# Stick-breaking prompt attention: the scores' lead, the first value product of a group, and the places of sigmoids and gates in line

## The reference

```
def _sb_block(q, qpos, k, v, kpos):
    scale = HEAD_DIM ** -0.5
    z = jnp.einsum('bqhd,bkhd->bhqk', q, k, preferred_element_type=jnp.float32) * scale
    causal = kpos[None, :] < qpos[:, None]
    log_keep = jnp.where(causal, jax.nn.log_sigmoid(-z), 0.0)
    rev = lax.cumsum(log_keep, axis=log_keep.ndim - 1, reverse=True)
    after = jnp.concatenate([rev[..., 1:], jnp.zeros_like(rev[..., :1])], axis=-1)
    log_a = jnp.where(causal, jax.nn.log_sigmoid(z) + after, -jnp.inf)
    a = jnp.exp(log_a)
    o = jnp.einsum('bhqk,bkhd->bqhd', a, v.astype(jnp.float32))
...
            h = (jax.nn.silu(z) * o.reshape(b, T, D_ATTN)) @ b_w_out[j]
```

## Time and profile before

| | |
|---|---|
| median of 3 runs | 2952.95 us (2952.86 to 2952.97) |
| the profiled execution | 2958.83 us, of which its span is 2957.2 us |
| PE busy over the span | 2848.7 us, 96% |
| DVE, ACT, POOL busy | 1652.0, 1344.4, 1159.3 us |
| attention, first score to last value product | 1453.7 to 2664.6 us |
| one pair in the middle (heads 6 and 7) | 1933.3 to 2087.6 us |

### The profile page before, as it was taken

How to read it: one execution, slowest core, us unless ns; L and a number is a source line. 1 busy time by engine, 2 the same in 40 slices (tenths; PEclk the granted TensorE clock), 3 DMA queues, 4 the chain that set the end, 5 groups by cost and what they waited for, 6 DMA issues and landing times. The chain is left out here.

```text
span 2957.2 us, 42069 instructions
## 1 busy us (share of the span) xinstructions
PE 2848.7 (96%) x14856; PEld 2470.5 (84%) x14856; DVE 1652.0 (56%) x2150; ACT 1344.4 (45%) x2746; POOL 1159.3 (39%) x1023
## 2 busy tenths in 40 slices
PE   7999999999999999999999999999999999998998
PEld 6999999999888888899788888888888877777886
DVE  5322123212443511022488888888888899897774
ACT  6000010100134511111377777777777788785442
POOL 3333233332110110022367666666667576662010
PEclk9999999999999999999999999999999999999999
DMA  5011111011344344244786767675767677857773
GB/s 159 30 33 33 36 36 34 24 36 37 116 150 128 118 173 177 105 148 158 219 243 182 229 183 230 185 226 177 235 176 221 201 213 223 258 182 214 238 226 112
DMA packets 286311, 451.16 MB, mean 153 GB/s; under 512 B 52898, under 2 KB 223010, under 8 KB 280132
## 3 DMA queue, kind: packets, MB, share of 16 engines
q1 hardware_dynamic: 275108, 409.23, 45.5%
q0 software_dynamic: 11040, 39.86, 4.5%
HBM read 325.22 MB, written 123.81 MB: 152 GB/s over the span
## 5 line engine op out<-in xcount | busy, mean ns | idle before, releaser
L1731 POOL TENSOR_TENSOR a_a<-a_a,a_prod 128x512 f32<-128x512 f32 (+3 forms) x640 | 664.8, 1049 | 423.1 <-DVE a_prod L1681 286.7
L1681 DVE TENSOR_TENSOR_SCAN a_prod<-a_keep,a_prod,a_restart 128x513 f32<-128x513 f32 x384 | 488.6, 1273 | 0.1
L1691 DVE TENSOR_TENSOR a_atl<-a_pt,a_ath 128x512 fp32r<-128x512 f32 (+3 forms) x640 | 380.4, 599 | 128.6 <-ACT a_ath L1631 125.1
L1621 ACT ACTIVATE a_a<-a_pz 128x512 f32<-128x512 f32 (+3 forms) x640 | 352.5, 551 | 179.2 <-PE a_pz L1544 166.4
L1631 ACT ACTIVATE a_ath<-a_pt 128x512 fp32r<-128x512 f32 (+3 forms) x640 | 349.2, 556 | 96.2 <-PE a_pt L1569 94.9
L1569 PE MATMUL a_pt<-ident,a_a 128*128 128x128 f32 x2176 | 346.1, 275 | 12.3 <-DVE a_atl L1691 6.9
L1622 ACT ACTIVATE a_keep<-a_pz 128x512 f32<-128x512 f32 (+3 forms) x640 | 354.0, 553 | 0.0
L1569 PEld LDWEIGHTS a_pt<-ident,a_a 128*128 128x128 f32 x2176 | 274.8, 141 | 69.6 <-POOL a_a L1731 14.9
L1554 PE MATMUL a_po<-a_ath,a_v 128*128 128x512 f32 (+3 forms) x640 | 288.8, 451 | 41.8 <-DVE a_atl L1691 21.2
L1543 PE MATMUL a_pz<-a_kh,a_q 128*128 128x512 f32 (+3 forms) x640 | 240.9, 378 | 11.8 <-ACT a_keep L1622 9.4
L277 POOL TENSOR_TENSOR w_wh<-w_raw,w_gain 128x1024 fp32r<-128x1024 f32 x22 | 42.1, 1911 | 536.1 <-PE v_pg L347 279.9
(11 more groups left out here) (233 smaller groups left out, 6079.1 us busy)
## 6 DMA issues: line engine op xcount, KB each, us to landing
a_x<-x_d SPq DMA_DIRECT2D x96, 896.0 KB, 4.7
a_x<-x_d SPq DMA_DIRECT2D x64, 832.0 KB, 4.7
a_kh<-kh_t SPq DMA_DIRECT2D x32, 512.0 KB, 10.8
a_kl<-kl_t SPq DMA_DIRECT2D x32, 512.0 KB, 14.2
w_raw<-in_a_w_in POOLq DMA_DIRECT2D x30, 512.0 KB, 4.8
x<-f_xn POOLq DMA_DIRECT2D x17, 512.0 KB, 6.0
g_y_in<-sz_t SPq DMA_DIRECT2D x17, 512.0 KB, 7.6
g_x<-x SPq DMA_DIRECT2D x17, 512.0 KB, 3.7
```

The lines of the kernel that those rows point to most:

```text
L1621: act.activation(a[:, s, q, 0:w], pz[:, n % ZS, 0:w], ACT.Sigmoid, scale=SCALE)
L1681: dve.tensor_tensor_scan(prod[:, s, 0:w + 1][:, ::-1], keep[:, n % KS, 0:w + 1][:, ::-1], restart[:, 0:1].broadcast_to([P, w + 1]), prod[: ...
L1691: dve.tensor_tensor(atl[:, b % AS, c0:], pt[:, turn_slot(hh, b), c0:], ath[:, b % AS, c0:].bitcast(F32), ALU.subtract).then_inc(at_split, 1)
L1731: pool.tensor_tensor(part, part, prod[:, n % PS, after:after + w], ALU.mult).then_inc(weighted, 1)
```

## The change

The lead goes from 3800 to 4300 columns, so PE's scores stand 500 columns (about one piece of 512) further ahead. How far each engine's part is put back is now in two tables: for score work ACT goes from 0 to 150, DVE stays at 600, POOL goes from 900 to 200, SP stays at 1000; for gates ACT and DVE go from 300 to 250, SP from 1000 to 1500. The product of the first block of each query group stands three blocks behind the transposes instead of two, directly ahead of the product of the second block. The chunks are moved: they begin at column 800 instead of 0 in an ordinary pair (2250 instead of 2000 in the pairs that only have the gate projection), and the last one stands nearer the pair's end. Nothing that is computed changes, nor any count of instructions.

```diff
-LEAD = 3800
-PE_AT, ACT_AT, DVE_AT, POOL_AT, SP_AT = 0, 0, 600, 900, 1000
+LEAD = 4300
+BEHIND = {"PE": 0, "ACT": 150, "DVE": 600, "POOL": 200, "SP": 1000}
+GATE_BEHIND = {"PE": 0, "ACT": 250, "DVE": 250, "POOL": 0, "SP": 1500}
...
+def begins_group(b):
+
+    return is_diagonal(BLOCKS[b][0]) and BLOCKS[b][1] == 0
+
...
-    first = 300 if is_pair(pr, 0) else 2000 if gates(pr) == (Z,) else 0
-    end = HEAD if is_pair(pr, NPAIR - 1) else 2 * HEAD - 1500
-    return [(first + (k + 0.5) * (end - first) / len(out), *x) for k, x in enumerate(out) if x[2] < PARTS]
+    first = 2250 if gates(pr) == (Z,) else 800
+    end = HEAD if is_pair(pr, NPAIR - 1) else 2 * HEAD - 750
+    return [(first + (k + 0.9) * (end - first) / len(out), *x) for k, x in enumerate(out) if x[2] < PARTS]
...
-            items.append((at + (300 if behind < SP_AT else 1000), 3, "gate", m, gx))
+            items.append((at + gate_behind, 3, "gate", m, gx))
...
-                before = lagged(pr, hh, b, LAG)
-                if before:
-                    multiply(*before)
+                for lag in (LAG + 1, LAG):
+                    before = lagged(pr, hh, b, lag)
+                    if before and begins_group(before[2]) == (lag > LAG):
+                        multiply(*before)
```

More of the change, by code:

```diff
@@ L1249, in chunks, with schedule @@
     out = [(gx, m, part) for gx in range(len(PGROUPS)) for m in gates(pr) for part in range(PARTS + 1)]
-    first = 300 if is_pair(pr, 0) else 2000 if gates(pr) == (Z,) else 0
-    end = HEAD if is_pair(pr, NPAIR - 1) else 2 * HEAD - 1500
-    return [(first + (k + 0.5) * (end - first) / len(out), *x) for k, x in enumerate(out) if x[2] < PARTS]
-def schedule(pr, behind):
+    first = 2250 if gates(pr) == (Z,) else 800
+    end = HEAD if is_pair(pr, NPAIR - 1) else 2 * HEAD - 750
+    return [(first + (k + 0.9) * (end - first) / len(out), *x) for k, x in enumerate(out) if x[2] < PARTS]
+def schedule(pr, who):
     last = is_pair(pr, NPAIR - 1)
+    behind, gate_behind = BEHIND[who], GATE_BEHIND[who]
     end = 2 * HEAD - 1
@@ L1399, in lagged, with all_pairs @@
             return None if is_pair(pr, 0) else (pr - 1, 1, N_BLOCK + b - k)
-        def all_pairs(eng, behind, do):
-            for what, hh, n in schedule(-1, behind):
+        def all_pairs(who, do):
+            for what, hh, n in schedule(-1, who):
                 if what == "score ahead":
@@ L1407, in all_pairs, with one_pair @@
             for pr in range(NPAIR):
-                one_pair(pr, behind, do)
-        def one_pair(pr, behind, do):
-            for what, hh, n in schedule(pr, behind):
+                one_pair(pr, who, do)
+        def one_pair(pr, who, do):
+            for what, hh, n in schedule(pr, who):
                 if what == "score ahead":
@@ L1521, in _ @@
             load_v(0, 1)
-            all_pairs(sp, SP_AT, do)
+            all_pairs("SP", do)
         @block.tensor
@@ L1604, in do @@
                     chunk(pr, *hh, n)
-            all_pairs(pe, PE_AT, do)
+            all_pairs("PE", do)
             for b in range(N_BLOCK - LAG, N_BLOCK):
@@ L1659, in do @@
                     project_out(pr, hh, n)
-            all_pairs(act, ACT_AT, do)
+            all_pairs("ACT", do)
             for b in range(N_BLOCK - LAG, N_BLOCK):
@@ L1717, in _ @@
             dve.wait_ge(restart_set, 2)
-            all_pairs(dve, DVE_AT, do)
+            all_pairs("DVE", do)
         @block.gpsimd
@@ L1777, in _ @@
                 pool.sem_inc(done, 2)
-            all_pairs(pool, POOL_AT, do)
+            all_pairs("POOL", do)
     return o_sb
```

## The result

The changed kernel takes 2902.51 us (median of 4 runs, 2899.85 to 2905.56) against 2952.96: a ratio of 0.9825, with a 95% interval of 0.9808 to 0.9842. That is -50.5 us where -27 was forecast; the time lies just under the lower end of the range and within 3 us of the first rival (2905). The direction and most of the places were right; the sum was about half of what came.

What follows compares the result with a forecast made beforehand. PE was taken as the bound, DVE close behind. Pairs 1 to 5 -13.1, pair 0 -2.9, pairs 6 and 7 -4.4, clock -6.8 made -27.2 us: 2952.95 to 2926; own range 2911 to 2944, with rivals 2904 to 2955.

Steps and rivals of the forecast that it cites:

- first rival: Whole kernel: more waits and clock falls go than the forecast counts, -48 us to 2905; chance 0.12.
- product 19, odd heads: Block 19 of odd heads: a gate and scan no longer stand ahead of it on DVE; 5 x 1.5, -7.5 us.
- short scores of group 0: Short scores of group 0: a chunk between them ends PE's waits for sigmoids, -6.1 us.
- short scores in blocks 28 to 30: Odd heads, next head's short scores: the 512-wide score waits for sigmoids behind ACT's copies; 5 x 1.5, +7.5 us.
- end of an even head: Products 37 and 38: block 38 moves ahead of a scan, a gate behind block 37; 5 x -0.7, -3.5 us.
- end of a pair and start of the next: Pair ends: the scan wait goes, missing fill adds 0.9; 1.6 instead of 2.1 us each, -2.5 over five.
- ACT's place costed at nothing: Stretches between the diagonal ones: scores keep the same gap between blocks on PE, ACT and DVE; cost nothing.
- sigmoids rival: Stretches of short scores: PE stands for sigmoids that ACT runs later, +20 us to 2973; chance 0.13.
- SP costed at nothing: SP's queue: gate stores move 500 columns back, some 2 us, and loads behind are asked for later; nothing.
- Clock: Clock falls: four of seven go, the start's, one behind block 19, two at pair ends; 4 x 1.7, -6.8 us.
- rival in which the clock falls more often at head ends: A fall at each of 16 head ends makes the clock term +15.3 instead of -6.8 us, 2948; chance 0.08.
- Pair 0: Pair 0: POOL wait at block 8 goes (-2.1), a chunk runs behind (+1.2), other terms -2.0; sum -2.9 us.

Runs made afterwards that it cites:

- e9: The kernel before with ACT's score work put 150 columns back and nothing else; ratio 0.9932 to the kernel before.
- e7: The changed kernel with ACT's score work back at 0 columns behind instead of 150; ratio 0.9909 to the kernel before.
- e13: The changed kernel with the old chunk places and SP's six key and query loads 2600 columns later in its line; ratio 0.9821 to the kernel before.
- e5: The changed kernel with the old chunk places; ratio 0.9887 to the kernel before.
- e6: The changed kernel without the deferral, a group's first product back at two blocks; ratio 0.9824 to the kernel before.
- e12: The changed kernel with the lead back at 3800 columns; ratio 0.9932 to the kernel before.
- e14: The changed kernel with POOL's score work back at 900 columns behind; ratio 0.9842 to the kernel before.
- e3: The kernel before with the lead at 4300 columns and nothing else; ratio 0.9967 to the kernel before.

## Why the prediction was wrong

**The size of pairs 1 to 5.** The forecast was -13.1 of waits and most of -6.8 of clock; measured were -32.5 and -6.8 (four falls, all of those pairs). The step that failed above all is the one that costed ACT's new place at nothing; beside it the sum was made from a list that holds too little, and the pair end was judged by DVE's busy share. By place, on PE's own list (us over pairs 1 to 5, rounded):

| place | before | forecast | measured change |
|---|---|---|---|
| product 19, odd heads | 7.4 | -7.5 | -7.4 |
| short scores of group 0 | 6.1 | -6.1 | -6.1 |
| short scores in blocks 28 to 30 | 0 | +7.5 | +3.4 |
| end of an even head | 5.9 | -3.5 | -5.9 |
| end of a pair and start of the next | 10.7 | -2.5 | -7.1 |
| other first products | 2.1 | -1.0 | -2.1 |
| x loads | 2.1 | 0 | +0.3 |
| sum | 34.2 | -13.1 | -24.9 |

*The list.* The sum was made from PE's list, 34.2 us, and PE's busy time was taken for work. The weight loads' list of the same stretch had 54.1, 20 us more, and fell by 32.5, 7.6 more than PE's own.

*ACT's place costed at nothing.* "On PE, ACT and DVE a score stands in the same gap between two blocks as before" was true where a gap is 512 columns wide, and I let it stand for the whole. The 150 columns of ACT appear in my text only as the cause of the slower rival. Alone they are worth more than any other part tried (e9: 0.68%), and 0.82% in the whole (e7): at the narrow blocks and at gates they put ACT's short copy ahead of the pair of sigmoids. The changed kernel without them (e7) is what I had forecast for all of it: 0.9909, some 27 us less than before, with 21.4 us left on PE's list, 12.8 less than before. That both sums meet so well is in part luck, since the terms behind them differ, and since parts do not add up here it does not make the 150 columns the whole error. But undone they cost 0.82%, 24 us, and 23 us is what the forecast lacks. The sigmoids rival's own mark, `a_keep` waits above 15 us, did not come: they went from 6.1 to 3.4 on PE's list. DVE's 1.68 us for ACT's gate stood in the earlier trace rows and I used it for one place alone; there were 30 such waits.

*The pair end.* 2.1 us were to become 1.6, since no chunk is left there and DVE was the bound. Measured is one wait of 0.55 for the accumulator and, at product 2 of the new head, one of 0.22:

```profile
2052.75 0.51 PE L1561 MATMUL a_po<-a_ath,a_v 128*128 128x512 f32 x1 [0.55 <-ACT a_o L1649]
2058.86 0.39 PE L1561 MATMUL a_po<-a_ath,a_v 128*128 128x256 f32 x1 [0.22 <-DVE a_atl L1699]
```

The same kernel without ACT's 150 (e7) has there, beside 0.54, still 0.70 at transposes 0. The 0.9 that I added for missing fill was too much. With the old chunks there (e13) the weight loads' waits from the transposes of block 38 to product 2 of the new head are 1.8 us a pair (0.59 and 0.97 for `a_atl`, 0.23 for `a_o`), without them 2.2 (0.79 and 0.39 for `a_o`; 0.20, 0.37 and 0.45 for `a_atl`), and on PE's list they are 0.9 and 0.8: the fill moved the waits more than it covered them. What bounded the stretch was ACT's and DVE's order.

Two sums of the range were wrong as well. The pair end's upper value of 4.0 counts the 0.9 twice (0.7 + 2.4 is 3.1), and the lower end, all of it taken together, is 2913 and not 2911.

**Short scores.** +1.5 in one odd place per pair was forecast; the place was right to the block, its price 0.7 us, 3.4 over five pairs instead of 7.5. The old ones at group 0 went, as said.

**SP costed at nothing.** Right for the changed kernel and wrong as a reading of it: an x load needed 18 us behind six key loads, and the chunks at a pair's start were held off only by the waits themselves (the earlier trace rows has 2.1 us already, at the third chunk of two pairs) and, with the change, by the 1000 columns that its chunks moved. I had costed that move as harmful. Undone, it costs 0.60% (e5), and e13 shows that the loads are why. Even so the changed kernel keeps 2.2 us of waits for x, now at the first chunk.

**The deferral.** "Hardly helps" was right: e6 shows no loss. "POOL, nothing" is not contradicted: 0.15% is below what the runs tell. The lead was costed at nothing, and that was wrong: alone it is worth 0.33%, and undone it costs 1.05% (e12). Among what comes back are the 0.98 us at the transposes of block 0 in each pair. I had that wait in the sum, as a scan ahead of block 38, but did not say that it is the lead that moves this scan; no wait for POOL came in pairs 1 to 5.

**Clock.** Two falls left instead of three, five fewer: -8.5 instead of -6.8. That this is so near is in part luck: the start's fall, which I let go, stayed, all those behind waits at head ends went, and a new one came in pair 7. The rival in which the clock falls more often at head ends is not borne out: the stretch around a pair's end still consists of transposes, short products and scores, with no chunk, and no fall stands in pairs 1 to 5. What went with the falls are the waits. The Trainium skill (TensorE: Matmul & The Clock Gate, Part 4: PE-mode transpose) says that a transpose does not count as PE-busy in the same way. No run here shows whether it does; by itself it made no fall at these ten head ends.

**Pair 0** gave 8.3 instead of 2.9, pair 6 5.7 and pair 7 0.7 instead of 4.4 together. The second POOL wait of pair 0 is gone as said, but not by what I said: without POOL's new place (e14) only 0.5 of its 2.1 us are back, and pair 0 takes 150.4 us instead of 149.8. The lead alone (e3) brings pair 0 from 158.0 to 153.4. Pair 7 has the new wait of 2.6 us for x in it, and the fall behind that wait. The rest was not split.

**The rivals.** 0.12 was given to "more goes than I count", whose 48 us are close to the 50 that came. Its argument against was DVE's 10.10 of 11.4 us: a busy share around the stretch, which said nothing on whether PE had to wait for DVE's next item or for a later one.

## What to carry to other kernels

When engines run fixed orders and the bound engine stands at narrow items, look first at what long item stands ahead of the short one it needs, on each engine of the chain; moving it takes no more work, and here one number on ACT was worth 0.7 to 0.8%. Price such a change from the weight loads' waits as well as from the matmuls', compare the two lists before believing the name of a releaser, and price parts together: one wait removed may uncover another (a late load) that was hidden behind it, so here a part that was worth nothing alone was worth 0.6% in the whole, and one that was worth 0.3% alone was worth nothing. When a load is late, look at what stands ahead of it in its queue. A wait on an engine with slack is no cost, but making its result later is one, as the late gate showed.

## What the runs showed of the hardware

The busy time of matmuls in the profile is not a constant of the work: with 4155 and 4160 matmul records it was 736.4 and 721.9 us in the two kernels, and only 6.8 of the 14.5 us between them are clock; the others are waits that the weight loads' list has and the matmuls' list has not (32.5 - 24.9 = 7.6). Loads of x of 896 KB landed 4.9 us after their issue in the median of e5, and needed 16 to 18 us behind 3 MB of other loads on the same queue (15.9 at pair 4 of the changed kernel, 17.7 at pair 2 of e5), 10.9 behind 3 MB whose issue had begun 3.4 us earlier (pair 7).
